# Moving the mixer gate's conditioning matvec out of the softmax rounds into the level stage of a Trainium2 encoder kernel

## What is computed

```python
c_act = jax.nn.silu(c)
shift, scale, gate = adaln(c_act, ada_w[layer, 0], ada_b[layer, 0])   # c_act @ w + b, split in three
h = x * (1.0 + scale) + shift
y = even_mixer(h, ...)                        # layer 0
x = layer_norm(ALPHA * x + (1.0 + gate) * y, ln_g[layer, 0], ln_b[layer, 0])
```

## Time and profile before

| | us |
|---|---|
| median of 3 runs | 2962.78 (2958.91 to 2967.27) |
| the profiled execution's own time | 2959.23 |
| its span, first to last instruction | 2957.4 |
| PE busy | 2665.2 (90%) |
| DVE busy | 1923.5 (65%) |
| ACT busy | 1073.4 (36%) |
| POOL busy | 128.9 (4%) |
| granted clock, mean | 0.946 |

### The profile page before, as it was taken

The page is one execution under the profiler, slowest core; times in us unless marked ns, Lnnn a source line. Parts: engine busy times, 40 slices in busy tenths (PEclk is TensorE's granted clock), DMA queues, the critical chain, the costliest instruction groups (busy, mean ns, idle before and its releaser), DMA issues.

```text
span 2957.4 us, 41913 instructions
## 1 busy us (share of the span) xinstructions
PE 2665.2 (90%) x16522; PEld 2154.3 (73%) x16522; DVE 1923.5 (65%) x1948; ACT 1073.4 (36%) x858; POOL 128.9 (4%) x201
## 2 busy tenths in 40 slices
PE   6969999976769899999999976859979999999997
PEld 3438888733458688888888862548868888888886
DVE  7956666657935777677777756746676665555555
ACT  3333333343223333333444422023433333344442
POOL 1020000000000200000000021010020000000000
PEclk9989999977879999999999988979989999999999
DMA  7988878622235488787878759468837777555551
GB/s 249 349 269 271 288 257 288 214 72 69 73 109 176 170 277 273 257 286 262 285 261 293 279 158 227 157 174 276 284 124 230 235 231 236 187 195 187 184 185 57
DMA packets 289270, 639.65 MB, mean 216 GB/s; under 512 B 76370, under 2 KB 79316, under 8 KB 285588
## 3 DMA queue, kind: packets, MB, share of 16 engines
q1 hardware_dynamic: 239236, 584.44, 59.7%
q0 software_dynamic: 11008, 35.99, 4.1%
q10 hardware_dynamic: 38928, 17.86, 2.2%
HBM read 614.24 MB, written 19.79 MB: 214 GB/s over the span
## 4 chain that ended last, share of the span: by engine, by line
PE 79%; DVE 12%; ACT 3%; ACTq 2%; issue 2%; DMA 1%; SPq 1%; DVEq 0%
PE PS L267 46%; PE PS L268 23%; PE PS L220 2%; ACT Pb L939 2%; DVE Pb L1693 2%; DVE acc L1688 1%; PE PS L885 1%; ACTq L983 1%; PE PS L184 1%; PE PS L714 1%; DMA omat<-WF 1%; DVE wlo L257 1%; DVE HF L1612 1%; ACTq L416 1%; PE PS L735 1%
## 5 line engine op out<-in xcount | busy, mean ns | idle before, releaser
L267 PE MATMUL PS<-H,whi 128*128 128x512 f32 x5888 | 2077.1, 398 | 102.0 <-DVE wlo L257 78.1
L268 PE MATMUL PS<-H,wlo 128*128 128x256 f32 x5888 | 1653.1, 281 | 0.0
L267 PEld LDWEIGHTS PS<-H,whi 128*128 128x128 f32 x5888 | 1112.3, 189 | 369.5 <-DVE wlo L257 84.5
L257 DVE TENSOR_TENSOR wlo<-raw,whi 128x2048 fp32r<-128x2048 f32 x368 | 843.6, 2293 | 735.3 <-ACT whi L253 734.8
L253 ACT ACTIVATE whi<-raw 128x2048 fp32r<-128x2048 f32 x368 | 705.3, 1918 | 1255.9 <-PE PS L268 1215.1
L268 PEld LDWEIGHTS PS<-H,wlo 128*128 128x128 f32 x5888 | 1118.6, 190 | 0.0
L176 DVE SCALAR_TENSOR_TENSOR acc<-araw,cact,acc 128x1024 f32<-128x1024 f32 x240 | 307.4, 1281 | 1.4 <-DMA araw<-in_ada_w 1.0
L939 ACT ACTIVATE Pb<-PS 128x1024 f32 (+5 forms) x117 | 118.3, 1035 | 162.1 <-issue 75.8
L939 ACT ACTIVATE H<-Pb 128x512 fp32r (+2 forms) x142 | 95.1, 670 | 41.6 <-DVE Pb L1358 27.7
L1406 DVE TENSOR_TENSOR H<-Pb,H 128x512 fp32r<-128x512 f32 x128 | 87.6, 684 | 0.0
L1302 DVE TENSOR_TENSOR raw<-Pb,HF 128x1024 f32<-128x1024 f32 x64 | 74.1, 1220 | 9.9 <-DMA omat<-WF 7.0
(11 more groups left out here) (258 smaller groups left out, 1406.0 us busy)
## 6 DMA issues: line engine op xcount, KB each, us to landing
raw<-in_mlp_w SPq DMA_DIRECT2D x256, 1024.0 KB, 5.8
araw<-in_ada_w SPq DMA_DIRECT2D x276, 512.0 KB, 4.5
raw<-in_mix_w_in SPq DMA_DIRECT2D x64, 1024.0 KB, 7.7
raw<-in_s_w_glu SPq DMA_DIRECT2D x32, 1024.0 KB, 7.4
acc<-in_ada_w SPq DMA_DIRECT2D x44, 512.0 KB, 7.0
raw<-in_ada_w POOLq DMA_DIRECT2D x32, 512.0 KB, 4.1
raw<-in_mix_w_out SPq DMA_DIRECT2D x16, 1024.0 KB, 5.1
vmat<-Pb ACTq DMA_DIRECT2D x8, 1024.0 KB, 7.5
```

The costliest lines, as they stand in the source:

```text
L257: nc.vector.tensor_tensor(wlo[:, s % 2, :], raw[:, s, :], whi[:, s % 2, :].bitcast(F), ALU.subtract).then_inc(S("lo_done"), 1)
L267: nc.tensor.matmul(PS[:, b, :], w[0], H2[:, :, k, :], start=first, stop=False, skip_group_check=True)
L268: return nc.tensor.matmul(PS[:, b, 0:T], w[1], H2[:, 0, k, :], start=False, stop=last, skip_group_check=True)
```

## The change

The call of `gate_part` in the softmax rounds is taken out, and GATE_SPLIT gets nine bounds in steps of four, so that levels 0 to 7 run four pieces each behind their scores. The order of the pieces, their buffers, their loads and what waits for them are the same.

```diff
-    GATE_SPLIT = (16, 18, 20, 22, 24, 26, 29, 32)
+    GATE_SPLIT = (0, 4, 8, 12, 16, 20, 24, 28, 32)
@@ attention_pe, end of a round
                     last.then_inc(S("at_pv"), 1)
-                    gate_part(pe, n)
                 rms_pe(pe, 1)
@@ hgrn_pe, behind the scores of a level
                     last.then_inc(S("lv_mm"), 1)
-                    if lv < 7:
+                    if lv < 8:
                         for c in range(GATE_SPLIT[lv], GATE_SPLIT[lv + 1]):
                             gate_part(pe, c)
```

## The result

The changed kernel takes 2972.95 us (median of 16 runs), the kernel before 2958.72 (16 runs, taken beside it). The ratio is 1.0053, 95% interval 1.0037 to 1.0068, so the change makes the kernel slower by 11 to 20 us; the two medians differ by 14.2. The profiled executions' spans are 2973.1 and 2957.4 us, but single executions differ by more than what is looked for here (the 16 of the kernel before lie between 2947 and 2967). What can be compared more finely is the length of a stage between two instructions of one profiled execution, and the rest of this text goes by that.

A forecast was written before the change was run, and what follows sets the result against it. VectorE was taken to bound the levels, a TensorE-VectorE ring the rounds, TensorE the stage's end. Rounds +6.9, levels 0 to 5 0, end +7.8 summed to +14.7 us; forecast 2976 us, range 2967 to 2985.

The forecast's parts named there:

- The direct gain in the rounds: Softmax rounds: without pieces, the late waits of rounds 8 and 10 fall to the bare ring, 1.4 us gained.
- The clock in the rounds: Softmax rounds: without pieces TensorE stays at 1.2 GHz, each ring goes from 1.24 to 2.00 us; sum +6.9 us.
- The first rival: Softmax rounds: clock stays high without pieces, so rounds gain 1.4, end costs 7.8: +6.4 us, 2969; chance 0.18.
- round 9's piece: Softmax rounds: piece after the values matmul delayed by logarithms, run at the low clock; round 10's wait 2.49 us.
- The cover of the first norm's sums: After the rounds: sums of 3.62 us may double at the low clock, but their ScalarE reader starts later; nothing lost.
- Levels 0 to 5: Added pieces make TensorE's work grow by 3.4 us where two are added, covered by VectorE; 0, bounds 0 and +2.
- The loads: POOL's 28 buffer refills, 4.1 us to landing, 12.5 at most, arrive in time for the pieces; 0.
- The end: Levels 6 to 8: level 7's four pieces and the PSUM chain delay level 8's scores; +7.8 us, bounds +7 and +10.
- The term for level 7: Between level 7's and level 8's scores: four pieces of 6.9 us plus the exposed copy out of PSUM, 0.8 us.
- a rival with 0.12: Dearer end: low clock in level 6 (+1.6) or behind level 8, or a late refill (up to +5); +19 or so, 2981.
- L816 in levels 1 to 6 near 3.9 us: Sign to look for: the levels' scores matmuls take near 3.9 us rather than 5.4.
- The output weights: Loads before the output projection come 10.5 us later, but their first reader moves too; nothing lost.

The follow-up runs named there:

- e3: The changed kernel plus two matmuls of a gate piece's shape in each softmax round, result unread; ratio 1.0029 to the kernel before.
- e1: The changed kernel (no pieces in the rounds) with levels 0 to 6 taking 5, 5, 5, 5, 5, 4, 3 pieces, none behind level 7; ratio 1.0028 to the kernel before.
- e2: The kernel before, rounds' pieces kept, with one piece fewer in levels 3 and 4, two fewer in level 5, four behind level 7; ratio 1.0033.
- e4: The kernel before with levels' pieces as 3, 3, 3, 3, 2, 2, 0, 0 and the turn moved ahead of level 7's scores; ratio 0.9979.
- e5: e4 plus unread constant-tile matmuls on TensorE around the two norms and ahead of the output projection; 2943.61 us, ratio 0.9954 to the kernel before.
- e6: The changed kernel plus one unread matmul of a piece's shape in each round, instead of e3's two; 2966.33 us in one execution.

## Why the prediction was right

The forecast was +14.7 us; the medians say +14.2, and 2972.95 lies within the range. The 2976 that I named is 3 us high because the kernel before came out at 2958.7 in 16 runs, not at 2962.8 as in three. Step by step:

**The direct gain in the rounds, -1.4.** Not contradicted: in round 10 the wait fell from 2.49 to 2.01, and round 8's extra 0.17 is gone. It appears only netted against the clock, as it was priced; no run has the rounds without pieces at the high clock, so it was never seen by itself.

**The clock in the rounds, +6.9 in all.** Right in mechanism and size: 7.1. All rounds at 0.50, every ring at 2.00, one round's loss absorbed at the logarithms (1.57 to 0.80). The first rival, that the clock stays high in bursts without a piece, was wrong; e3 shows that it is the clock that carries the cost and e1 that nothing from the levels is needed for it. What the working said of round 9's piece alone holds for more: in the kernel before the clock also fell in rounds 3, 5, 7 and 11, and there too the piece took the low stretch. The rule of the Trainium skill, "TensorE: Matmul & The Clock Gate", on oscillation in real kernels, is that waits between bursts can drop the clock each time, so that each burst starts slow. In the changed kernel each burst did start slow, in all fourteen rounds, but the clock was not dropped anew each time: it stood at 0.50 over the whole stretch of 91.70 us.

**The cover of the first norm's sums.** Right: they ran partly at the low clock, and VectorE's wait for the spread was 2.38 us as before, so nothing came through.

**Levels 0 to 5, 0.** Nearly: TensorE's extra work is covered, as is its lateness of 0.5 us behind level 0. But these levels grew by 0.42 us, by a term that the sum did not have: five of the six puts took 2.47 to 2.54 us instead of 2.42, which is 0.43 us in all. It lay within the bound of +2.

**The loads.** Right: refills took 5.0 us to landing in the median instead of 4.1, and no piece waited (each level's sixteen instructions took 7.03 us). That it is because four are asked for in a row now is likely but not shown.

**The end, +7.8.** The term for level 7 was exact: 7.77, and e2 gives it alone. Level 6 was mis-sized: I had its scores at the high clock, with +1.6 for the low one kept as a bound and as a rival with 0.12. They ran mostly at the low clock in the profiled execution, and level 6 to level 7 grew by 1.69. Also of what should be seen, "L816 in levels 1 to 6 near 3.9 us" held in four of six; levels 3 and 6 took 5.4. The argument that denser work would hold the clock was right only where TensorE rests little: it stood still 2.1 us ahead of level 6's scores, which took 5.41, but as long ahead of level 5's, which took 3.81. The profiled executions of the changed kernel, e3, e4, e5 and e6 have fourteen rests of 2.0 to 2.1 us ahead of a level's scores; behind seven of them the scores took 5.4 us, behind seven 3.8. So the clock is a chance of its own there, which the sum should have carried at half of 1.6 us.

**The output weights, 0.** Right: counted from level 0's scores, they were issued 12.8 us later and read 10.6 us later. They took 9.5 us to land for 8.9, and 43.6 us lie between the issue and the first reader, so nobody waited. The delay was more than the 10.5 us that I gave; my own terms there make some 10.8, and level 6's clock and the puts add 2.1.

**The total** is a little lucky. The stage grew by 17.6 us in the profile, the medians by 14.2 with an interval of 11 to 20. Of the 17.6, 0.7 lie behind level 8, where the first value products ran at the low clock (+1.5) and the second norm's sums were shorter (-0.8). I had said that no later stage moves: from the output projection to the end the two profiled executions take 2092.4 and 2095.7 us, and up to round 0's transposes the changed one is 5.2 us shorter, with the same code in both; differences of that size between single executions are scatter and show neither.

## What to carry to other kernels

Matmul work that fits into the gaps of a loop bound by a ring through other engines is not neutral there: in this loop it brought TensorE's clock back each time that it had fallen, and so kept it up for most of the ring's own short matmuls. Taking it out made the loop slower by 7.1 us with less to do, and putting back work that nobody reads made it faster again by 6.9. A stage's last steps are the wrong place for filler: there the ring is over, everything waits for TensorE, and the pieces cost their full length plus the chain behind them (7.8 us for 6.9 of work). So fill where another engine sets the period, stop one or two steps ahead of the end (e4, 3.3 us of stage), and look at the matmuls behind TensorE's idle stretches, since they may run at half speed (the spread before: 7.19 us, and 3.71 in e5).

## What was not expected of the hardware

VectorE's masked copy out of PSUM (L1612 before, 128x2048) takes 2.42 us where TensorE is still and mostly 0.1 us more where gate pieces reach into it: in the kernel before once (2.52 at 807.99, beside level 6's pieces), in the changed kernel in six of seven such puts (2.47 to 2.54; the seventh took 2.42), in e4 once, behind level 0 (2.50). In all eight kernels the puts that ran beside pieces from start to end took 2.48 to 2.54 us, and those that met none took 2.42; those that met some for a part of their time (0.3 to 2.2 us) took 2.42 to 2.52. Whether it is PSUM, which both then use, or the reading side was not separated.

The second thing is how well the length of the rounds repeats. The rounds take 114.77 and 114.76 us in the two kernels without pieces, and 107.68, 107.83, 107.73 and 107.92 in the four that have two matmuls there (before, e2, e4, e3), each another execution and begun at another time. In e5, whose rounds are the same, the long waits fall on other rounds (2.18 in round 1, 1.43 in round 5, 1.72 in round 10, 1.79 in round 11), and the fourteen still sum to 20.2 us as before.
